# Moving one tile's mixer transpose to another PSUM bank, with its waits and its place in three queues

## The reference

```
p = h @ w_in                                   # one projection for three groups of heads
A = latent attention (8 heads) over the prompt, and over 8192 cached rows for the samples
B = RWKV-7 time mixing (4 heads of 64): S <- S(diag(w) - kk^T (a*kk)) + v k^T ; y = S r
    out = (group_norm(y) * g + b + bonus) * gate
C = gate_b * conv3(gate_c * u)
h = LN(alpha*h + concat(A, B, C) @ w_out)
h = LN(alpha*h + HierMoE(h))                   # top 2 of 8 experts in 1 of 4 groups
```

## Time and profile before

| | before |
|---|---|
| median of 3 executions | 3140.44 us (3137.47 to 3149.29) |
| profiled execution | 3137.47 us, span 3135.3 us |
| busy share of the span | PE 87%, PEld 49%, DVE 45%, ACT 25%, POOL 21% |
| mean granted TensorE clock | 0.934 of full speed |
| chain that ended last | PE 75%, DVE 10%, DMA 5%, ACT 3%, issue 3%, DVEq 3% |
| DMA | 503.08 MB, mean 160 GB/s |

### The profile page before, as it was taken

How to read it: one execution, slowest core, us unless ns; L and a number is a source line. 1 busy time by engine, 2 the same in 40 slices (tenths; PEclk the granted TensorE clock), 3 DMA queues, 4 the chain that set the end, 5 groups by cost and what they waited for, 6 DMA issues and landing times.

```text
span 3135.3 us, 56735 instructions
## 1 busy us (share of the span) xinstructions
PE 2742.0 (87%) x22522; PEld 1530.6 (49%) x22522; DVE 1426.4 (45%) x3976; ACT 791.0 (25%) x1875; POOL 653.7 (21%) x651
## 2 busy tenths in 40 slices
PE   6998899999979959999399988989999898699980
PEld 3545566666645523333145456666666455233320
DVE  4112677766643452222450047667665335322227
ACT  0101255555522001111110024455555120011110
POOL 1000011111100035455310011111110000455533
PEclk9998899999989979999699979999999898799995
DMA  7113242332242449898741123423322326499956
GB/s 282 57 46 97 61 126 91 96 98 90 86 138 69 192 141 361 336 361 289 275 153 50 38 87 93 128 92 95 104 90 73 111 99 242 167 367 361 360 191 225
DMA packets 171843, 503.08 MB, mean 160 GB/s; under 512 B 48412, under 2 KB 89376, under 8 KB 146368
## 3 DMA queue, kind: packets, MB, share of 16 engines
q1 hardware_dynamic: 101760, 307.91, 28.6%
q0 software_dynamic: 50240, 120.23, 11.1%
q10 hardware_dynamic: 19584, 71.31, 5.8%
HBM read 629.93 MB, written 86.89 MB: 229 GB/s over the span
## 4 chain that ended last, share of the span: by engine, by line
PE 75%; DVE 10%; DMA 5%; ACT 3%; issue 3%; DVEq 3%; SPq 0%; POOL 0%; ACTq 0%; POOLq 0%
PE ps L820 68%; PE ps L817 7%; DMA c_x<-xd 2%; DMA xs<-pd 1%; DVE S_all L2656 1%; DVE grams L2192 1%; ACT PT L1664 1%; DVE c_x L2228 1%; ACT kT L1664 1%; DMA c_b<-ybd,dga 1%; DMA ybd<-yb 0%; ACT S_all L1920 0%; DVE c_h L2206 0%; ACT PT L1948 0%; DVE negm L2658 0%
## 5 line engine op out<-in xcount | busy, mean ns | idle before, releaser
L820 PE MATMUL ps<-w_slots,xbT 128*64 128x512 f32 (+1 forms) x2048 | 458.6, 601 | 18.6 <-DVE xbT L3132 18.6
L820 PE MATMUL ps<-hT,w_in 128*128 128x512 f32 x896 | 390.2, 597 | 4.1 <-ACT hT L1664 4.1
L747 POOL DMA_INDIRECT xb<-xd,idall x256 | 256.9, 1004 | 152.9 <-issue 80.7
L820 PEld LDWEIGHTS ps<-w_slots,xbT 128*64 128x64 f32 x2048 | 144.1, 138 | 287.5 <-issue 268.6
L820 PE MATMUL ps<-w_out,o_mixT 128*128 128x512 f32 x576 | 262.6, 604 | 18.9 <-issue 17.6
L820 PEld LDWEIGHTS ps<-hT,w_in 128*128 128x128 f32 x896 | 170.9, 192 | 216.7 <-issue 210.8
L820 PE MATMUL ps<-w_slots,hidT 128*64 128x512 f32 (+1 forms) x1024 | 235.1, 598 | 9.3 <-issue 7.8
L3132 DVE STREAM_TRANSPOSE xbT<-xb 128x1024 f32<-128x1024 f32 x64 | 79.7, 1245 | 347.1 <-DMA xb<-xd,idall 332.2
L820 PE MATMUL ps<-grams 64*64 64x64 f32 (+1 forms) x4624 | 174.5, 222 | 29.2 <-DVE grams L2192 22.0
L820 PEld LDWEIGHTS ps<-grams 64*64 64x64 f32 (+1 forms) x4624 | 154.3, 136 | 56.6 <-issue 25.8
L1664 ACT ACTIVATE kT<-ps 128x512 f32<-128x512 f32 x256 | 138.7, 593 | 146.3 <-PE ps L817 145.9
(11 more groups left out here) (395 smaller groups left out, 4281.7 us busy)
## 6 DMA issues: line engine op xcount, KB each, us to landing
w_slots<-in_w_gu SPq DMA_DIRECT2D x64, 2048.0 KB
w_slots<-in_w_dn SPq DMA_DIRECT2D x64, 1024.0 KB
ybd<-yb ACTq DMA_DIRECT2D x64, 512.0 KB
pd<-stage SPq DMA_DIRECT2D x56, 256.0 KB, 2.5
out_y<-c_h ACTq DMA_DIRECT2D x27, 512.0 KB, 2.9
w_in<-in_w_in SPq DMA_DIRECT2D x6, 2048.0 KB, 25.5
o_mixT<-mixd SPq DMA_DIRECT2D x18, 512.0 KB, 4.2
o_h<-out_y SPq DMA_DIRECT2D x18, 512.0 KB, 4.8
```

The lines of the kernel that those rows point to most:

```text
L747: pool.indirect_dma_start(xb[p % 2][:, 256 * q:256 * q + 256], None, x_quarters, bass.IndirectOffsetOnAxis(ap=idall[:, NE * q + p:NE * q + ...
L820: return pe.matmul(out, lhsT, rhs, start=start, stop=stop, skip_group_check=True)
```

## The change

PE's mixT of slots 1 to 7 writes the upper half of bank K[1] instead of Q[2]. It no longer waits for ACT's copy of head 5; it waits for DVE's copy of sq(0) of tile i, the last reader of K[1]. sq(1), which writes K[1] next, waits for ACT's copy of mixT. pt(6,0) waits for the copy of head 5 like any other head. On DVE rr(0) is put ahead of yn. On ACT p(7) is put ahead of mixT. The sample tile keeps Q[2], and tile 7, which had K[1] before, keeps it. No instruction is added or taken away.

More of the change, by code:

```diff
@@ L185 @@
 ACT_S0 = "2ssq 1sq1 2th 1sq2 1off1 1off2 1mv 1wt 2lora 2gate 2mlaT 2exps 2qn 2kn 1mixT 2V 2qrT 2tokm 2sq0 2sq1 2sq2 2off1".split()
-DVE_A = "1hnx 2gramD 2gram23 2sq0 2gram4 1yn 2rr0 2sq1 2rr1 2sq2 2rr2 2off1".split()
+DVE_A = "1hnx 2gramD 2gram23 2sq0 2gram4 2rr0 1yn 2sq1 2rr1 2sq2 2rr2 2off1".split()
 DVE_S = ("kkx logs qn qr kk2 rkv qrT gramD gram23 new sq0 gram4 rr0").split()
@@ L1081, in sq @@
                     W = self.W
+                    if r == 1 and self.seam:
+                        pe.wait_ge(act_a.sem, act_a.at(("a", self.l, self.i - 1), "mixT"))
                     if r:
@@ L1205, in mixT @@
                     pe.wait_ge(dve_a.sem, dve_a.at(self.k, "yn"))
[L1206 to L1209, removed]
+                    if self.i + 1 < NPT:
+                        pe.wait_ge(dve_a.sem, dve_a.at(("a", self.l, self.i + 1), "sq0"))
+                    out = Q[2] if self.sample else K[1][:, 256:512]
                     for f in range(2):
@@ L1248, in pt @@
                         pe.wait_ge(act_b.sem, act_b.at(self.k, f"p{h}"))
-                        if h == 6 and self.i + 1 < NPT:
-                            pe.wait_ge(act_a.sem, act_a.at(("a", self.l, self.i), "mixT"))
-                        elif h:
+                        if h:
                             pe.wait_ge(act_b.sem, act_b.at(self.k, f"pt{h - 1}.{int(self.nk > 4)}"))
@@ L1907, in mixT @@
                     act.wait_ge(mixC_out, 16 * self.n)
-                    self.done(cp(mixC[:, 0:2, :W], v3(K[1][:, 256:512] if self.i + 1 == NPT else Q[2], 2)[:, :, :W]), "mixT")
+                    self.done(cp(mixC[:, 0:2, :W], v3(Q[2] if self.sample else K[1][:, 256:512], 2)[:, :, :W]), "mixT")
             class Att:
@@ L2040, in slot @@
                 t.pt(5, 1)
+                t.p(7)
                 w.mixT()
-                t.p(7)
                 x.sq(1)
@@ L2869, in slot @@
                 x.gram4()
+                x.rr(0)
                 w.yn()
-                x.rr(0)
                 t.s(7)
```

## The result

The kernel with the change takes 3194.53 us (median of 4 executions, 3191.00 to 3197.45), the kernel before 3141.86 us (median of 4). The ratio is 1.0165, 95% interval 1.0142 to 1.0187: it is slower by 1.65%, or 45 to 59 us. The profiled execution took 3192.24 us with a span of 3190.0 us, 54.8 us more than that of before. The forecast was 3183 us, 11.5 us too low.

What follows compares the result with a forecast made beforehand. PE bounds the kernel, busy 465.57 of 513 us. Delays of sq(1), less 0.62 us in each of slots 1 to 3, sum to 21.4 us a layer, 42.8 us in two: 3183 us, own range 3174 to 3192, wider 3167 to 3208.

Steps and rivals of the forecast that it cites:

- last sign: Sign that the prediction is wrong: the clock after sq(1) on PE is below 1.
- The delay of sq(1): PE's sq(1) waits for rr(0), yn, s(7), p(7) and the copy: 3.12 us late in slot 1, 3.52 in 4, 3.23 in 7.
- The unseen link: ACT's copy of mixT releasing PE's sq(1), not shown by the trace: priced 0.14 us, together with the copy 0.52 us.
- mixT's wait for DVE: On PE ahead of mixT in slot 1: a wait of some 2 us for DVE's mix.
- yn's lost cover: On DVE, yn goes behind rr(0) and is no longer hidden while PE computes rr(0); its four operations take 1.83 us.
- The two removed waits of PE: Ahead of mixT and pt(6,0): at most 0.18 + 0.17 = 0.35 us a slot, taken as nothing.
- Rival 3: The shared bank Q[2] held PE and ACT; the split removes 14 x 0.35 = 4.9 us: 3135.5 us; chance 0.06.
- The clock stays at 1.00: PE's clock does not fall after sq(1), as after stands up to 2.1 us in layer 0; the forecast's chance 0.66.
- Rival 2: PE's clock falls at the new gap before sq(1): 49 us more in all 14 slots, 3232 us; half, 3208; chance 0.14.
- The price of a fall: A fall of PE's clock from 2.4 to 1.2 GHz costs 3.5 us, from slot 3 of layer 1.
- rival 1: Load xs lands by traffic: slots 1 to 3 hide 9.7 us more, slow clock regains 3.5: 3170 us; chance 0.14.
- What xs gives back: In slots 1 to 3, xs moves only with ACT's mixT copy, so 0.62 us less each, 6 x 0.62 = 3.7 us.

Runs made afterwards that it cites:

- e1: Kernel after the change with DVE's order as before (yn ahead of rr(0)), ACT's order and the bank still changed; 3173.78 us, ratio 1.0097.
- e3: Kernel after the change with DVE's and ACT's orders as before, so only mixT's bank and its waits changed; 3154.39 us, ratio 1.0034.
- e2: Kernel after the change with ACT's order as before (copy of mixT ahead of p(7)), DVE's order and the bank still changed; 3183.71 us, ratio 1.0127.
- e4: Kernel before the change with SP's store of mixC moved behind the loads; 3126.34 us, ratio 0.9956.
- e6: Kernel after the change with SP's store of mixC moved behind the loads; 3199.02 us, ratio 1.0176.
- e8: Kernel after the change with four useless PE transposes ahead of mixT, four behind it, and SP's store of mixC behind the loads; 3181.33 us, ratio 1.0126.
- e9: Kernel after the change with useless PE transposes filling each slot's stands and SP's store of mixC behind the loads; 3161.95 us, ratio 1.0096.
- e5: Kernel after the change with four useless PE transposes ahead of mixT and four behind it; 3195.61 us, ratio 1.0167.
- e7: Kernel after the change with PE's pv(2) and pt(6,0) moved ahead of mixT and sq(1); 3190.19 us, ratio 1.0151.
- e10: Kernel after the change with useless PE transposes filling each slot's stands, SP's order unchanged; 3174.00 us, ratio 1.0131.

## Why the prediction was nearly right, and which of its steps failed

The number came out by luck. By the forecast's own last sign it is wrong, since the clock after sq(1) is below 1. Two of its terms failed, in opposite directions.

**The delay of sq(1): right.** Predicted were 3.12, 3.52 and 3.23 us in slots 1, 4 and 7; the profile has 2.96, 3.44 and 3.13. Summed over 14 slots it is 45.65 us where the forecast had 46.5 before its deduction. The unseen link, ACT's copy to PE, was priced 0.10 us too high: from the start of the copy to sq(1) it takes 0.42 us, not 0.52, and 1.4 us over 14 slots is enough for the difference.

**mixT's wait for DVE and yn's lost cover: right.** mixT waits 2.26 us in slot 1 (2 were predicted). e1 shows that DVE's order is 16 us of the delay, e3 that with both orders undone 7.6 us are left, ACT's copy alone between mixT and sq(1). The two removed waits of PE gave nothing, as costed. Rival 3, a gain by the split, is refuted by e3: the split by itself is slower (1.0020 to 1.0048).

**The clock stays at 1.00: wrong.** The forecast gave this most of its chance because a stand of up to 2.1 us had not lowered the clock in layer 0. Rival 2's event took place in all 14 slots and not in half of them. The Trainium skill, TensorE: Matmul & The Clock Gate, section "HAM oscillation — how this bites in real kernels", says of a kernel whose PE waits for its loads between short bursts that each next burst begins at the low clock. The trace of the kernel after agrees with it in 14 of 14 slots, those of e1 and e2 in 10 of 14; the two transposes in the middle did not protect.

**The price of a fall: too high.** The forecast took 3.5 us from one slot of the kernel before. The runs give 2.0 us (e4 and e6), 2.3 us (e6 and e8) and 2.0 us (slot by slot against e9), with 1.3 to 2.7 us for nearly all single falls. The clock rows say the same of the kernel after: 6 us times what the clock lacks of 1.00, summed over the 14 stretches, is 29.5 us of PE's time, 2.1 us each. So the falls cost 14 x 2.03 = 28.4 us, not 49.

**What xs gives back: too small, and rival 1's reason was not the one.** The forecast let each slot give back 0.62 us, 3.7 us in all, since only the copy's shift reaches SP. All 13.4 us were given back, with 3.5 us for the slow stretch of the earlier trace rows: 16.9 us, rival 1's 13.2 us on top of the 3.7. Rival 1 put it down to traffic. The rows show another cause. In slot 3 the load and its reader were, before and after:

```profile
559.49 0.43 SPq L521 DMA_DIRECT2D xs<-pd  x1
...
569.34 0.31 ACT L1787 ACTIVATE th<-xs 64x128 f32<-64x128 f32 x1 [1.92 <-DMA xs<-pd]
```

```profile
569.30 0.43 SPq L521 DMA_DIRECT2D xs<-pd  x1
...
580.71 0.30 ACT L1786 ACTIVATE th<-xs 64x128 f32<-64x128 f32 x1
```

Counted from rr(0) (553.06 and 560.45), the load is issued 2.42 us later, as the forecast has it (2.70). But th comes 3.98 us later: 3.40 for sq(1) and 0.58 more, because the work between sq(1) and th, which took 12.22 us without its wait, takes 14.72 us behind the fall. If the load takes as long as before, the delay alone hides 0.98 us of the wait of 1.92 (3.40 less 2.42), and the 2.50 us of slower work hide the rest. The slots 1 to 3 of the other kernels with the same delay and SP's old order (e5, e7, e10) bear it out. In the 8 of them in which the clock stayed at 1.00, th waits for xs in 7, 17.4 us in all; in the 10 in which it fell, th waits in 3, 3.9 us in all, and in the kernel after, with a fall in all 6, never. A part of the 17.4 us, 1.25 us in each of e10's four slots among them, is th being ready earlier there. So rivals 1 and 2 were no alternatives here; what rival 1 forecast followed from the fall of rival 2. That the load's issue matters is shown by e4, where it is issued earlier and all waits go.

**The sum again.** In the profiled executions: delay 45.6, falls 28.4, waits for xs -13.4, the slow stretch -3.5, together 57.1 us against 54.8 measured; the 2.3 us between are within what the sum is good for. The forecast's 42.8 us left out 28.4 and gave back 13.2 too little, which leaves 15 us; with the delay 0.9 us smaller than forecast and the 2.3 us that the sum has too many, these are the 12.0 us by which 54.8 exceeds 42.8. The times show 11.5. The forecast's own range of 3174 to 3192 us was missed by 2.5 us; the wider one, which takes in half of rival 2, holds the time. The price of the falls in the two slots 7 is taken from the others.

## What to carry to other kernels

A wait inserted ahead of PE costs its length and, if PE's clock falls behind it, some 2 us more for each time in this kernel; the granted clock right behind the wait and the number of matmuls tell, since PE looks fully busy there (6.00 of 6.00 us with 91 and with 131 matmuls). A load's wait is not a fixed sum to be given back: it is the gap between two chains, and anything that slows one chain alone, a clock too, eats it. The cheap gain was found by asking what stands ahead of a late load in its queue: moving one store behind it made the kernel 0.44% faster (0.26 to 0.61%), with no change to the work.

## What the hardware did that was not expected

The length of a single stand does not decide whether the clock falls. In the kernel before, in slot 2 of layer 1, PE stands 2.79 us ahead of the next transposes, and over the 6 us behind it the clock is 1.00:

```profile
2039.74 1.06 PE L817 MATMUL ps<-cst,ckvr 128*128 128x128 f32 x8 [2.79 <-ACT kT L1664]
```

```profile
2039.74:2045.74 6.00, 6.00 (x80) 4.10 (x82) 3.63 (x15) 4.12 (x12) 0.49 (x1) 1.00 0.02 4
```

In e1 a stand of 1.93 us was followed by 0.72, in e2 stands of 1.62 and 0.47 us with two transposes between them also were, and 8 transposes (e5, e8) left 5 falls of 14. Of PE's stands behind a late xs, those of 3.25 us (e10) and more were all followed by 0.50 to 0.62 over 6 us, and one of 3.00 us (e3) by 1.00.

Nor do the instructions around the stand decide it. In e1 slot 7 has the same steps in both layers and the same stand of 2.64 us ahead of sq(1). In layer 0 the clock over the next 6 us is 0.50 and PE does 64 matmuls, in layer 1 it is 1.00 and PE does 103:

```profile
879.96 1.97 PE L820 MATMUL ps<-grams 64*64 64x64 f32 x32 [2.64 <-ACT mixC L1663]
```

```profile
879.96:885.96 6.00, 6.00 (x64) 5.35 (x64) 0.42 (x1) 0.38 (x1) 0.00 (x0) 0.50 0.19 60
```

```profile
2437.24 1.15 PE L820 MATMUL ps<-grams 64*64 64x64 f32 x32 [2.64 <-ACT mixC L1663]
```

```profile
2437.24:2443.24 6.00, 5.33 (x103) 4.65 (x103) 1.29 (x4) 1.47 (x3) 0.00 (x0) 1.00 0.19 60
```

Slot 1 of e1 shows it the other way round, with a stand of 1.46 us: 1.00 in layer 0, 0.50 in layer 1. What decides a single case was not settled, so how many of 14 slots fall can't be read from the length of a stand or from the program alone.

A second thing stays open. In e4 the copy of off1, the step behind rr(2), begins 2.48 us behind PE's start of that step in slot 1 (432.08 and 434.56), in e9 1.20 us (438.47 and 439.67). That is why th is ready 1.25 us earlier there and in e10. The instructions around that step are the same, and the slots of e9 are not shorter for it. No run was made on it.
